# Two feed-forwards of a decoder step in fp32: block products by Strassen's scheme in place of whole matrix products

## What is computed

```
D_MODEL, SEQ, DEC_BATCH, DEC_SEQ, DEPTH, D_FF, CONV_W = 1024, 1024, 8, 4, 2, 2816, 3

def conv_ffn(x, g, w_in, conv_w, conv_b, w_down, prefix):
    t = x.shape[1]
    gu = rms_norm(x, g) @ w_in
    a, up = jnp.split(gu, 2, axis=-1)
    full = jnp.concatenate([prefix, a], axis=1)
    c = conv_b + sum(conv_w[r] * full[:, r:r + t] for r in range(CONV_W))
    y = (jax.nn.silu(c) * up) @ w_down
    return y, full[:, -(CONV_W - 1):]
...
        x = x + jnp.concatenate([o, xo], axis=-1) @ w_out
        yf, cst = conv_ffn(x, p['norm2_g'][i], p['w_ffn_in'][i], p['conv_w'][i],
                           p['conv_b'][i], p['w_down'][i], prefix)
        x = x + yf
```

## Time and profile before

| | us |
|---|---|
| Device time, median of 3 runs (2229.9 to 2232.53) | 2231.43 |
| Profiled execution: span from first to last instruction | 2229.1 |
| PE busy in it | 2210.4 (99%) |
| DVE busy | 1171.5 (53%) |
| ACT busy | 664.2 (30%) |
| POOL busy | 564.4 (25%) |
| DMA queue q1, share of 16 engines | 15.3% |

### The profile page before, as it was taken

One profiled execution on the slowest core, in us unless ns is written; L12 is line 12 of the kernel. 1 busy time (PEld: TensorE's weight loads), 2 busy tenths in 40 slices (PEclk: granted clock), 3 DMA queues, 4 the chain that ended last, 5 costly groups with the idle time before them and its releaser, 6 DMA issues.

```text
span 2229.1 us, 39205 instructions
## 1 busy us (share of the span) xinstructions
PE 2210.4 (99%) x15290; PEld 2138.2 (96%) x15290; DVE 1171.5 (53%) x2164; ACT 664.2 (30%) x1208; POOL 564.4 (25%) x433
## 2 busy tenths in 40 slices
PE   9999999999999999999999999999999999999999
PEld 8997689999999999999999997999999999999999
DVE  8356751745545455444575256165545455454554
ACT  6315962412221112221253226142221112221121
POOL 1004634312221122221252223432221122221121
PEclk9999999999999999999999999999999999999999
DMA  5224001111111011110111130111111011110112
GB/s 195 81 100 149 3 24 42 53 39 48 56 56 38 28 47 56 56 38 30 49 48 61 46 106 32 40 38 57 57 56 37 29 47 56 56 38 28 48 56 92
DMA packets 39425, 123.63 MB, mean 55 GB/s; under 512 B 5388, under 2 KB 13572, under 8 KB 38536
## 3 DMA queue, kind: packets, MB, share of 16 engines
q1 hardware_dynamic: 36504, 113.45, 15.3%
q10 hardware_dynamic: 2832, 8.94, 1.1%
HBM read 115.78 MB, written 8.63 MB: 56 GB/s over the span
## 4 chain that ended last, share of the span: by engine, by line
PE 91%; ACT 3%; DVE 2%; issue 1%; POOL 1%; DMA 1%; SPq 0%; DVEq 0%; ACTq 0%; POOLq 0%
PE ps L676 29%; PE ps L677 29%; PE ps L678 29%; ACT s_exp L1480 1%; PE ps L1066 1%; DVE h_lo L1787 1%; PE ps L1021 1%; PE ps L856 1%; PE ps L1047 1%; ACT p_t L1265 0%; DMA x<-in_x_t 0%; ACT h_hi L1325 0%; ACT x_sq L1361 0%; PE ps L987 0%; POOL s_exp L612 0%
## 5 line engine op out<-in xcount | busy, mean ns | idle before, releaser
L676 PE MATMUL ps<-h_hi,w_hi 128*128 128x352 f32 x3120 | 1012.6, 325 | 3.9 <-DVE h_lo L1787 3.5
L677 PE MATMUL ps<-h_lo,w_hi 128*128 128x352 f32 x3120 | 1000.2, 321 | 0.0
L678 PE MATMUL ps<-h_hi,w_lo 128*128 128x352 f32 x3120 | 999.8, 320 | 0.0
L497 POOL TENSOR_TENSOR w_lo<-raw,w_hi 128x1024 fp32r<-128x1024 f32 x118 | 298.4, 2529 | 1462.6 <-ACT w_hi L1265 1462.6
L676 PEld LDWEIGHTS ps<-h_hi,w_hi 128*128 128x128 f32 x3120 | 585.2, 188 | 15.7 <-issue 6.5
L677 PEld LDWEIGHTS ps<-h_lo,w_hi 128*128 128x128 f32 x3120 | 586.4, 188 | 0.7
L678 PEld LDWEIGHTS ps<-h_hi,w_lo 128*128 128x128 f32 x3120 | 584.8, 187 | 0.0
L2207 DVE TENSOR_TENSOR x<-x,ps 128x352 f32<-128x352 f32 x528 | 270.9, 520 | 170.4 <-PE ps L678 169.6
L676 PE MATMUL ps<-g_hi,d_hi 128*128 128x352 f32 x1056 | 340.2, 322 | 0.0
L677 PE MATMUL ps<-g_lo,d_hi 128*128 128x352 f32 x1056 | 339.9, 322 | 0.0
L678 PE MATMUL ps<-g_hi,d_lo 128*128 128x352 f32 x1056 | 339.7, 322 | 0.0
(11 more groups left out here) (211 smaller groups left out, 1688.1 us busy)
## 6 DMA issues: line engine op xcount, KB each, us to landing
raw<-in_w SPq DMA_DIRECT2D x181, 512.0 KB, 3.7
s_mk<-in_s_mk SPq DMA_DIRECT2D x2, 2048.0 KB, 9.3
s_mv<-in_s_mv SPq DMA_DIRECT2D x2, 2048.0 KB, 13.8
out_y<-x ACTq DMA_DIRECT2D x7, 528.0 KB
x<-in_x_t SPq DMA_DIRECT2D x2, 1408.0 KB, 11.8
mem_x<-in_mem_t SPq DMA_DIRECT2D x1, 1024.0 KB, 7.8
s_k<-in_s_k SPq DMA_DIRECT2D x2, 512.0 KB, 4.1
s_v<-in_s_v SPq DMA_DIRECT2D x1, 1024.0 KB, 16.0
```

What stands on the lines that cost most here:

```text
L497: pool.tensor_tensor(lo, raw[:, slot], hi.bitcast(F32), ALU.subtract).then_inc(prepped, 1)
L676: pe.matmul(out, a, hi_x(k), start=(first and n == 0), stop=False)
L677: pe.matmul(out, a, lo_x(k), start=False, stop=False)
L678: ins = pe.matmul(out, b, hi_x(k), start=False, stop=(last and n == len(ks) - 1))
```

## The change

Each product of the feed-forward is done as seven products of half blocks, in the form with chained sums (Winograd's variant). The weight matrix is cut in 2 x 2 blocks A11, A12, A21, A22, the activations in B11, B12, B21, B22 (halves of the inner dimension and halves of the tokens, 528 each), and PE computes the products of A11, S1, S2, S4, S3, A12, A22 with B11, T1, T2, B22, T3, B21, T4. S1 to S4 and T1 to T4 are sums or differences of blocks:

- **Gate and up of all tiles first.** 22 pairs (`NPAIR`) of two units with the same seven activation operands, which stay in SBUF. A pair is 7 products of 4 k-tiles x 2 chunks of 264 tokens x 3 = 24 matmuls of 128x264, 168 in all, where the same two units were 144 matmuls of 128x352. The even pairs are gates, the odd ones ups; `i` is a gate pair and the up pair behind it.
- **Weights.** POOL makes the four sums S of a pair (`sum_block`, L799, 128x512) and all seven low parts (`low_block`, L784, 128x512), ACT the seven high parts. `w_hi` and `w_lo` are rings of four blocks; `w_sum` lies in the same bytes as `w_lo`. Raw weights have three buffers (`raw` and `raw2`), of which a pair takes two.
- **PSUM.** Three slots of two banks. `CHAIN` gives the slot of each product; the fourth to seventh product of a pair add onto what an earlier one left. DVE takes a slot's value after products 1 to 6 (`taken`), ACT copies product 0 (`copy_first`), and PE waits for these before it adds on.
- **The product of gate and up** goes to DRAM: DVE forms the quarter blocks' sums for the down product (`g_sum`), SP stores seven blocks of 128x528 for each `i` (`store_g`), 1056 KB and 792 KB in two DMAs, and loads them for the down stage (`load_g`, 128x1056 each).
- **Down.** 5 groups (`NGRP`) of 4 hidden tiles, each with 4 pairs of output tiles. A pair is 7 products of 12 matmuls of 128x264, 84 in all, where it was 72 of 128x352. The blocks are 128x256, in rings of eight. The last two hidden tiles are left to `last_down`: 48 plain fp32 matmuls of 128x352 straight from the raw weights and `g_last`.
- **Entry.** The activation operands are built while the out projection adds to `x` (`early_operands`) and during the first pair; the norm's means and factors move into the first pair too.
- The loops of the feed-forward are written out, and some semaphores are shared between the layers.

The core of the diff (indentation cut by 8):

```diff
+HT, HC = T // 2, T // 4
+HK = KD // 2
+HB = HK * P
+POS = {"A11": 0, "S1": 1, "S2": 2, "S4": 3, "S3": 4, "A12": 5, "A22": 6}
+CHAIN = [0, 1, 2, 1, 2, 0, 2]
+DPOS = {"S2": 0, "A11": 1, "S1": 2, "S3": 3, "A12": 4, "S4": 5, "A22": 6}
+SPILL = {"B11": 0, "T4": 1, "B21": 2, "B22": 3, "T1": 4, "T2": 5, "T3": 6}
...
+def block_of(flat, j):
+    if j < NPROD * NPAIR:
+        return flat[:, HB * (j % 4):HB * (j % 4 + 1)]
+    at = DB * ((j - NPROD * NPAIR + 4) % 8)
+    return flat[:, at:at + DB].rearrange("p (m n) -> p m n", m=GPAIRS)
+def freed_by(j):
+    b = j - NPROD * NPAIR
+    return j - 4 if b < 0 else NPROD * NPAIR - 4 + b // 2 if b < 8 else j - 8
...
+    def ffn(l):
+        o0 = (O_OUTA, O_OUTB)[l]
+        sp.wait_ge(prepped, o0 + 7)
+        load_unit(l, 0)
+        sp.wait_ge(prepped, o0 + 8)
+        load_unit(l, 1)
+        sp.wait_ge(mx[l]["o_done"], past(l, "o_done") + KD * NCH)
+        load_unit(l, 2)
+        for v in range(3, 2 * NPAIR + 1):
+            if v >= 7 and v % 4 == 3:
+                store_g(l, (v - 7) // 4)
+            unit_freed(l, v - 3)
+            load_unit(l, v)
+        last = NPROD * (NPAIR - 1)
+        sp.wait_ge(spilled, 32 * ((NG - 1) * l + GPAIRS))
+        for k in range(NPROD):
+            sp.wait_ge(prod, done(l, last + (0, 1, 1, 2, 3, 4, 6)[k]))
+            load_g(l, 0, k)
+            if k in (1, 3):
+                unit_freed(l, 2 * NPAIR + (k + 1) // 2 - 3)
+                load_unit(l, 2 * NPAIR + (k + 1) // 2)
+        sp.wait_ge(spilled, 32 * (NG - 1) * (l + 1))
...
+    def low_block(l, j, name, v):
+        pool.wait_ge(w_cut, done(l, j))
+        whole = block_of(flat_sum, j) if name[0] == "S" else weight_part(name, v)
+        pool.tensor_tensor(block_of(flat_lo, j), whole, block_of(flat_hi, j).bitcast(F32), ALU.subtract) \
+            .then_inc(w_ready, 1)
...
+    def sum_block(l, pair, j, name, a, b, op, after=None):
+        slot_free(l, j)
+        if after is not None:
+            pool.wait_ge(w_summed, sums(l, pair, after))
+        pool.tensor_tensor(block_of(flat_sum, j), a, b, op).then_inc(w_summed, 1)
+    def pair_first(l, n):
+        j, v = NPROD * n, 2 * n
+        low_block(l, j, "A11", v)
+        pool.wait_ge(ffn_landed[(v + 1) % 3], raw_turn(l, v + 1))
+        sum_block(l, n, j + 1, "S1", weight_part("A21", v), weight_part("A22", v), ALU.add)
+    def pair_middle(l, n):
+        j, v = NPROD * n, 2 * n
+        sum_block(l, n, j + 2, "S2", weight_part("A11", v), block_of(flat_sum, j + 1), ALU.subtract, after="S1")
+        pool.wait_ge(w_summed, sums(l, n, "S2"))
+        low_block(l, j + 1, "S1", v)
+        sum_block(l, n, j + 3, "S4", weight_part("A12", v), block_of(flat_sum, j + 2), ALU.add)
+        pool.wait_ge(w_summed, sums(l, n, "S4"))
+        low_block(l, j + 2, "S2", v)
+        low_block(l, j + 3, "S4", v)
+    def pair_last(l, n):
+        j, v = NPROD * n, 2 * n
+        sum_block(l, n, j + 4, "S3", weight_part("A21", v), weight_part("A11", v), ALU.subtract)
+        low_block(l, j + 4, "S3", v)
+        low_block(l, j + 5, "A12", v)
+        low_block(l, j + 6, "A22", v)
...
+    def product(slot, j, xs, ks, first, last):
...
+        for c in range(2):
+            t0 = c * HC
+            out = ps[:, 2 * slot + c, 0:HC]
+            for k in ks:
+                begin, end = first and k == 0, k == len(ks) - 1
+                pe.matmul(out, hi_w[:, k, :], hi_x[:, k, t0:t0 + HC], start=begin, stop=False, skip_group_check=True)
+                pe.matmul(out, hi_w[:, k, :], lo_x[:, k, t0:t0 + HC], start=False, stop=False, skip_group_check=True)
+                mm = pe.matmul(out, lo_w[:, k, :], hi_x[:, k, t0:t0 + HC], start=False, stop=end,
+                               skip_group_check=True)
+        mm.then_inc(prod, 1)
+    def gate_up(l):
...
+            for pos in range(NPROD):
+                j = NPROD * n + pos
...
+                elif pos in (0, 2):
+                    pe.wait_ge(taken, before - (1 if pos == 0 else 0))
+                if pos in (3, 4):
+                    pe.wait_ge(taken, before + pos - 2)
+                if pos == 5:
+                    pe.wait_ge(p1_copied, NPAIR * l + n + 1)
+                if pos == 6:
+                    pe.wait_ge(taken, before + 4)
+                pe.wait_ge(w_ready, done(l, j))
+                product(CHAIN[pos], j, operands[pos], range(HK), pos in (0, 1, 2), True)
+                if n == 0 and pos == 2:
+                    norm_mean(w, 0)
+                    norm_mean(w, 1)
+                if n == 0 and pos == 4:
...
+    def down(l):
...
+        for p in range(DPAIRS):
+            g = p // NOP
+            before = NPROD * (DPAIRS * l + p)
+            slots = [down_slot(p), 0, 1, down_slot(p), 0, 1, down_slot(p)]
+            for pos in range(NPROD):
+                j = NPROD * (NPAIR + p) + pos
+                if p % NOP == 0:
+                    pe.wait_ge(g_ready, NPROD * (NGRP * l + g) + pos + 1)
+                if pos == 0 and p == 1:
+                    pe.wait_ge(taken, ends)
+                if pos == 0 and p >= 2:
+                    pe.wait_ge(added, before - NPROD)
+                if pos in (1, 2):
+                    if p == 0:
+                        pe.wait_ge(taken, ends - (1 if pos == 1 else 3))
+                    else:
+                        pe.wait_ge(added, before - NPROD + pos + 4)
+                if pos >= 3:
+                    pe.wait_ge(added, before + pos - 2)
+                pe.wait_ge(w_ready, done(l, j))
+                product(slots[pos], j, (g_hi[g % 2][pos], g_lo[g % 2][pos]), range(GPAIRS), pos < 3, True)
...
+    def last_down(l):
...
+        for q in range(KD * NCH):
+            oo, c = q // NCH, q % NCH
...
+                pe.wait_ge(std_added, KD * NCH * l + q - 4)
+            for f in range(2):
+                if q == 0:
+                    pe.wait_ge(ffn_landed[(v + f) % 3], raw_turn(l, v + f))
+                mm = pe.matmul(ps[:, std_bank(q), 0:CH], raw_unit(v + f)[:, oo * P:(oo + 1) * P],
+                               g_last[:, f, c * CH:(c + 1) * CH], start=(f == 0), stop=(f == 1))
+            mm.then_inc(std_done, 1)
...
+        def g_sum(i, t):
+            made = 4 * ((NG - 1) * l + i)
+            if t == 0:
+                dve.wait_ge(up_scaled, 3 * (NG * l + i + 1))
+                TT(t_buf[:, 0, :], c_buf[:, 0, second], c_buf[:, 0, first], ALU.subtract).then_inc(g_summed, 1)
+            if t == 1:
+                TT(t_buf[:, 2, :], c_buf[:, 0, second], c_buf[:, 1, second], ALU.subtract).then_inc(g_summed, 1)
+            if t == 2:
+                dve.wait_ge(g_summed, made + 1)
+                TT(t_buf[:, 1, :], t_buf[:, 0, :], c_buf[:, 1, second], ALU.subtract).then_inc(g_summed, 1)
+            if t == 3:
+                dve.wait_ge(g_summed, made + 3)
+                TT(c_buf[:, 0, second], c_buf[:, 1, first], t_buf[:, 1, :], ALU.add).then_inc(g_summed, 1)
...
+        def up_pair(i):
+            n = 2 * i + 1
+            finish_b(n - 1, i)
+            tap(i, 0, 1)
+            product_done(n, 1)
+            dve.wait_ge(spilled, 32 * ((NG - 1) * l + i))
+            p1_plus(n, 1, t_buf[:, 1, :])
+            tap(i, 0, 2)
+            product_done(n, 2)
+            p1_plus(n, 2, t_buf[:, 0, :])
+            tap(i, 1, 1)
+            product_done(n, 3)
+            parts_taken(n, 2)
+            plus(1, t_buf[:, 0, :])
+            tap(i, 1, 2)
+            product_done(n, 4)
+            plus(2, t_buf[:, 1, :])
+            scale(i, 0)
+            product_done(n, 5)
+            dve.wait_ge(c_scaled, NF * l + 2 * i + 1)
+            out = g_last if i == NG - 1 else c_buf
+            TT(halves_of(out[:, 0, first]), chain_banks(0), halves_of(c_buf[:, 0, first]), ALU.mult).then_inc(taken, 1)
+            scale(i, 1)
+            product_done(n, 6)
...
```

More of the change, by code:

```diff
@@ L104, with norm_bank @@
 NORM_BANK = [6, 7, 5]
+def norm_bank(w, c):
+    return NORM_BANK[c] if w % 2 == 0 else 6 + c % 2
 MEANS_AFTER = [1, 2, 9]
@@ L129, in item @@
     return kind, q, b + n % 2
-def down_bank(q, last):
-    return (3 + (q + 1) % 5) if not last else [0, 1, 2, 6, 7][q] if q < 5 else 3 + q % 5
 SAMPLE_AT = (8, 0)
@@ L465, in _ @@
+            stream(O_OUTA, O_OUTA + 2)
             m = mx[0]
@@ L1256, in _ @@
-                group(0, False, first=True)
-                with pe.Fori(1, NG - 1) as i:
-                    group(i, False)
-                group(NG - 1, True)
+                ffn(l)
         @block.scalar
@@ new lines, in high_block @@
+            def high_block(l, j, name, v):
+                if j < 4:
+                    act.wait_ge(proj, 3 * ((R_OUTA, R_OUTB)[l] + 7 + j // 2))
+                else:
+                    act.wait_ge(prod, done(l, freed_by(j)))
+                if name[0] == "S":
+                    pair = j // NPROD
+                    act.wait_ge(w_summed, sums(l, pair, name))
+                    whole = block_of(flat_sum, j)
+                else:
```

(24 more changed lines are left out.)

1023 lines of the change are left out of this document (660 added, 363 removed).

## The result

The changed kernel takes **2367.22 us**, the median of 4 runs (2359.09 to 2369.25), against 2231.69 (2229.9 to 2232.53, 4 runs) before: a ratio of 1.06, with a 95% interval of 1.0583 to 1.0617. It is 6% slower. I had forecast 2197, in a range of 2128 to 2270. The forecast was wrong in sign, and the time is above the slowest rival (2330).

The account below looks back on a forecast made before the run. PE bound the old kernel; in gate and up, POOL and DVE excluding each other would now. Span 2229.1 - 40 (gate/up) - 38 (down) + 11 (change of stage) + 22 (entry) + 11 (last tiles) = 2195; median 2197 us, range 2128 to 2270.

Parts of the forecast that it names:

- PE's step of 0.123 us at 264 tokens: Distance of PE's matmul starts: 0.1233 us at 264 tokens against 0.159 at 352; gate or up pair 20.7 us.
- 44.0 us per `i`: Gate and up: a gate pair plus up pair takes 44.0 us instead of 45.8, -40 us over 22.
- port: Gate and up: POOL and DVE operations with two SBUF operands exclude each other, so their times add.
- bounds of 40.3 to 44.3: Gate and up, per `i`: summed POOL and DVE times, 44.3 us by recorded durations, 40.3 with overlaps taken off.
- rival 2: Gate and up: second weight unit of up pairs loads late behind a store; `i` 47.3 us, median 2270, chance 0.24.
- Down stage, I take 10.5: Down stage: a pair takes 10.5 us against PE's limit of 10.36, -38 us over 40 pairs.
- DVE's adds are not in that path: Down stage: DVE's adds left out of the 10.4 us per pair summed from POOL's and DVE's work.
- Change of stage 5.5 us per layer: From up to down: PE waits for DVE's low parts of g and adds; bounds 3 and 14, +11 us.
- Entry 11 us per layer: First pair: DVE's reciprocals, operands and encounters with POOL exceed PE's time by 11 us; bounds 5 and 17, +22.
- Last two tiles 28.3 us: End of down: 48 fp32 products at 0.59 us each, 28.3 against 22.9 us, +11 for both layers.
- Free: Spill, weight and down loads, written-out loops and the out projection's extra DVE work were taken to cost nothing.
- Rival 3: Up pair: DVE's queue is the bound, 28.6 us against 20.7; `i` 50 us, median 2330, chance 0.05.

Follow-up runs that it names:

- e11: The kernel of e6 timed again in five runs against the kernel before: 2168.81 us, ratio 0.9719.
- e10: e6 with POOL's low parts of A11, A12 and A22 in gate and up cut to 16 of 512 columns, leaving the result incomplete: 2133.9 us.
- e8: The changed kernel with only DVE's low parts of the next g moved one to three products later in the down stage: 2282.8 us.
- e1: The changed kernel with ACT taking the next g's high part ahead of the weights' high parts in the down stage: 2300.0 us.
- e2: The changed kernel with POOL forming sum S3 ahead of S4 in the down stage: 2271.8 us.
- e6: The change with loads before stores, ACT's g before weights (down, change of stage), POOL's S3 before S4, DVE's low parts of g later: 2171.0 us.
- e7: e6 with POOL, at each feed-forward's entry, making the second product's sum and low part ahead of three additions of squares: 2170.5 us.
- e3: The changed kernel with SP issuing the next weight unit's load ahead of the store of g in gate and up: 2313.4 us.

## Why the prediction was wrong, by its own steps

- **PE's step of 0.123 us at 264 tokens: right.** From 1011.95 to 1012.07 it is 0.12, and a pair of gate or up units that waits for nothing takes 20.4 us (20.7 predicted), one of down 10.3 (10.36).
- **44.0 us per `i`: close, for the wrong reason.** It measured 45.0 (45.1 in layer 1). My 44.0 was all port, 2.6 us over PE's 41.4. What POOL's work costs turned out at 1.9 over PE's 40.9 in layer 0 and 1.1 in layer 1 (e11 against e10), inside the bounds of 40.3 to 44.3 once the load is in place. The other 2.2 (3.0) are the late weight unit, which I held apart as rival 2 and priced at 3.3 us over the forecast. The two are not alternatives: both were there, and the number came near since one priced too high made up for one left out. Of the signs, PE's waits were released by POOL's `w_lo`, as said; the taps had a median of 1.7 us, not near 2, and POOL was busy 79% of the pairs from 453 to 861, not 65 to 70%, since its held time counts as busy too. Cost of the step: 21 us over both layers.
- **"Down stage, I take 10.5": this step failed.** It measured 13.2 per pair from the third pair on (13.3 in layer 1), 99 us over both layers. The sums under it were right: with three queues reordered, the same work takes 10.3. What failed is the inference from "each engine's work is below PE's" and "rings of eight blocks" to "PE is full". I had counted the work of each engine, and never laid the four queues next to one another at one product and asked what stands behind each waiting instruction. "DVE's adds are not in that path" holds for the path that POOL and DVE share, but with it I left the adds out of the stage altogether: they stand behind `low_g` in DVE's queue, and PE waited 41.6 us for them in layer 0. They are one link of the ring and not the whole of it: with the low parts of g moved away from them alone (e8), the stage is still 243.
- **Change of stage 5.5 us per layer (bounds 3 and 14): failed.** The last gate/up product took 10.2 us instead of 2.9, and the first two down pairs 26.3 and 18.9 instead of 10.3 each: 32 us (29 in layer 1), 49 us over the forecast for both layers. The cuts of the ring shorten it: in layer 0 it is 22 us in e8, 19 in e1, 15 in e2 and 10 in e6. The last 10 are explained only in part.
- **Entry 11 us per layer: near.** The first two pairs took 35.1 and 22.9, 58.0 us against an `i` of 44.0: 14, inside the bounds of 5 and 17, and 6 us over the forecast for both layers. e7 (35.0) and e10 (33.2 for the first pair) left it nearly where it was; what sets it is open.
- **Last two tiles 28.3 us: right**, 28.1.
- **"Free": the loads and stores are free of bandwidth, not of order.** The order of SP's queue cost some 2.5 us per `i` (e3). 528 KB loads of g landed in 5.8 us in the median, and no row shows an engine's wait put down to them.
- **Rival 3 (DVE's queue is the bound)** named the right kind of thing, adds and takes queued behind blocked operations, but in gate and up, where an `i` took 45.0 us and not 50. It gave the time nearest to the result by luck, by another mechanism.

In sum, the down pairs, the change of stage, the `i` and the entry: 99 + 49 + 21 + 6 = 175 us, against the 172.5 by which the span missed.
